# A transformer front end whose adaLN modulation goes through TensorE as unsplit weights with two moving columns, and whose attentions are spread between the projections

## The reference, cut to what matters

```python
mod   = silu(c)     @ w_mod + b_mod          # (1, 6*1024): w_mod is 1024 x 6144
mod_c = silu(c_ctx) @ w_mod + b_mod
h  = rms_norm(x,   norm1_g) * (1 + mod[:, 1])   + mod[:, 0]      # 256 x 1024
hc = rms_norm(ctx, norm1_g) * (1 + mod_c[:, 1]) + mod_c[:, 0]
rq, rk, rv, rg, dq, dk, dv = split(h @ w_in)                     # w_in is 1024 x 3072
crq, crk, crv, crg, cdq, cdk, cdv = split(hc @ w_in)
ret  = rms_norm(retention(rope(rq), rope(rk), rv, crk, crv)) * silu(rg)    # 4 heads
diff = rms_norm((softmax(q1 k1) - lam * softmax(q2 k2)) @ [cdv; dv])       # 4 heads
#      with q, k = rope(rms_norm(dq)), rope(rms_norm(dk)), keys and values of ctx ahead
x = x + mod[:, 2] * (concat(ret, diff) @ w_out)                  # w_out is 1024 x 1024
# then: norm2 with mod[:, 3:5], product-key experts, mod[:, 5], and the second block
```

## Time and profile before

| | us |
|---|---|
| median of 3 runs | 1954.08 (1949.49 to 1954.12) |
| the profiled execution's own time | 1954.57 |
| its span | 1952.8 |
| first projection matmul starts | 60.2 |
| output projection starts, ends | 330.6, 354.2 |
| norm2 turned, queries follow from | 369.3 |

### The profile page before, as it was taken

How to read it: one execution, slowest core, us unless ns; L and a number is a source line. 1 busy time by engine, 2 the same in 40 slices (tenths; PEclk the granted TensorE clock), 3 DMA queues, 4 the chain that set the end, 5 groups by cost and what they waited for, 6 DMA issues and landing times.

```text
span 1952.8 us, 32582 instructions
## 1 busy us (share of the span) xinstructions
PE 1761.0 (90%) x13280; PEld 1550.8 (79%) x13280; DVE 1288.8 (66%) x2058; ACT 949.1 (49%) x1218; POOL 218.7 (11%) x100
## 2 busy tenths in 40 slices
PE   3788975799998999999999999899999678999997
PEld 1455744699898888999999989799989557799985
DVE  5769446589988999877775555555452766555555
ACT  6564433455444555444454444544454435554445
POOL 0123400162200000000000000000006344000000
PEclk8889977899998999999999999999998779999998
DMA  7445301344443444544454545445544122455541
GB/s 280 168 158 189 141 7 46 127 152 155 163 150 116 147 147 146 193 173 168 161 191 173 194 157 189 151 167 180 192 175 182 65 86 87 153 199 180 187 173 65
DMA packets 41958, 299.38 MB, mean 153 GB/s; under 512 B 4624, under 2 KB 4752, under 8 KB 6096
## 3 DMA queue, kind: packets, MB, share of 16 engines
q1 hardware_dynamic: 41296, 294.41, 41.8%
q0 software_dynamic: 512, 2.88, 0.4%
HBM read 295.18 MB, written 2.10 MB: 152 GB/s over the span
## 4 chain that ended last, share of the span: by engine, by line
PE 72%; DVE 20%; ACT 6%; issue 1%; DMA 1%; DVEq 0%; ACTq 0%; SPq 0%
PE pb L607 71%; DVE ar L1558 5%; DVE w_lo L1558 4%; ACT ar L1136 2%; DVE ar L1570 2%; ACT w_hi L1136 2%; DVE ar L1563 1%; DVE ar L1888 1%; ACT L1136 1%; DVE sm L1578 1%; DVE ar L1885 1%; DVE ar L1565 1%; DVE fsc L1565 1%; DVE ar L1574 1%; DVE ar L1892 0%
## 5 line engine op out<-in xcount | busy, mean ns | idle before, releaser
L1558 DVE TENSOR_TENSOR w_lo<-raw,w_hi 128x1024 fp32r<-128x1024 f32 x459 | 569.9, 1242 | 271.9 <-ACT w_hi L1136 250.8
L1136 ACT ACTIVATE w_hi<-raw 128x1024 fp32r<-128x1024 f32 x546 | 579.0, 1060 | 342.0 <-PE pb L607 319.6
L607 PE MATMUL pb<-HX,w_hi 128*128 128x256 f32 x3904 | 712.9, 285 | 4.8 <-DVE w_lo L1558 4.7
L607 PEld LDWEIGHTS pb<-HX,w_hi 128*128 128x128 f32 x3904 | 615.7, 193 | 10.6 <-DVE w_lo L1558 2.9
L607 PE MATMUL pb<-HX,w_lo 128*128 128x256 f32 x1952 | 553.9, 284 | 0.0
L607 PE MATMUL pb<-w_hi,HC 128*128 128x512 f32 (+1 forms) x1584 | 508.6, 392 | 4.5 <-DVE w_lo L1558 4.5
L607 PEld LDWEIGHTS pb<-HX,w_lo 128*128 128x128 f32 x1952 | 376.3, 193 | 0.0
L607 PEld LDWEIGHTS pb<-w_hi,HC 128*128 128x128 f32 x1584 | 298.4, 189 | 64.9 <-DVE w_lo L1558 5.5
L1558 DVE TENSOR_TENSOR ar<-ar 128x512 bf16<-128x512 bf16 (+6 forms) x464 | 276.2, 632 | 73.7 <-ACT ar L1136 54.2
L607 PE MATMUL pb<-w_lo,HC 128*128 128x512 f32 (+1 forms) x792 | 308.4, 389 | 0.0
L1136 ACT ACTIVATE ar<-pb 128x512 f32<-128x512 f32 (+2 forms) x237 | 139.3, 588 | 267.5 <-PE pb L607 198.0
(11 more groups left out here) (116 smaller groups left out, 817.0 us busy)
## 6 DMA issues: line engine op xcount, KB each, us to landing
raw<-in_wall SPq DMA_DIRECT2D x273, 1024.0 KB, 4.8
ar<-in_bigrows POOLq DMA_DIRECT2D x2, 1024.0 KB, 5.2
x<-in_x SPq DMA_DIRECT2D x1, 1024.0 KB, 12.6
ar<-in_ctx SPq DMA_DIRECT2D x1, 1024.0 KB, 14.3
ar<-in_dist SPq DMA_DIRECT2D x1, 1024.0 KB, 6.8
ar<-in_keys SPq DMA_DIRECT2D x1, 1024.0 KB, 4.8
x_keep<-x SPq DMA_DIRECT2D x1, 1024.0 KB, 3.8
x<-x_keep SPq DMA_DIRECT2D x1, 1024.0 KB, 8.3
```

Of the source, the lines that this page charges most:

```text
L607: return e.matmul(o, l, r, start=start, stop=stop, skip_group_check=True)
L1136: a.did(e.activation(out, in_, func, scale=scale, **kw), sig)
L1558: v.did(e.tensor_tensor(out, a_, b_, op), sig)
```

## The change

The modulation's weights are no longer split. Each block of 128 output features is eight plain f32 matmuls straight from `raw`: the stationary operand is a 128x128 piece of `w_mod`, the moving one is the two columns silu(c), silu(c_ctx) (`mod_block`). The result is already in columns, so `mrow`, its copies and its transposes go. There are 48 such blocks, 384 matmuls. Only the 24 projection halves (and all later ones) are split now, all of them in the front on VectorE; `reach` says how far the splitting may run ahead past unsplit halves.

The norm's factor is folded into the turning: x and ctx are multiplied with a scaled diagonal `dg4` in plain f32 (`first_turn`) instead of being scaled and transposed. The group order becomes 3, 4, 5, 0, 1, 2 (differential q, k, v first), and the head transposes, the rounds of differential attention, the masks and retention stand between projection halves and modulation blocks (`front_steps`). The output projection takes the differential half of `w_out` first, and retention's norm and transposes come in its middle.

```diff
-GROUPS = [3, 4, 0, 1, 5, 2]
+GROUPS = [3, 4, 5, 0, 1, 2]
...
+    mods(0, 12)
+    steps.append(("xturn", 0))
+    mods(12, 16)
+    steps.append(("gain", 0))
+    win(0, 0, ("cturn", 0))
+    win(0, 1, ("cturn", 1), ("cturn", 2), ("ctx", 0), ("ctx", 1))
...
+    win(2, 3, ("evac", 2), ("square", 5), ("unit", 5))
+    win(3, 0, ("kturn", 0))
+    mods(16, 18)
...
+    mods(22, 24)
+    steps.append(("score", 0))
+    win(3, 2, ("score", 1), ("turn", 0))
+    mods(24, 28)
+    steps.extend([("score", 2), ("weigh", 0), ("turn", 1)])
+    win(3, 3, ("evac", 3), ("score", 3), ("weigh", 1), ("turn", 2))
+    mods(28, 32)
+    steps.extend([("added", 1), ("score", 4), ("weigh", 2), ("turn", 3)])
+    win(4, 0, ("score", 5), ("weigh", 3), ("turn", 4), ("mask", 0))
+    win(4, 1, ("score", 6), ("weigh", 4), ("turn", 5), ("rope", 4))
...
+    win(5, 2, ("rscore", 0), ("dnorm", 0))
+    mods(32, 34)
+    win(5, 3, ("evac", 5), ("rscore", 1), ("rweigh", 0))
+    mods(34, 36)
+    steps.extend([("rscore", 2), ("rweigh", 1)])
+    mods(36, 38)
+    steps.extend([("rscore", 3), ("rweigh", 2)])
+    mods(38, 42)
+    steps.extend([("rweigh", 3), ("dblocks", 0)])
+    mods(42, 48)
+    steps.extend([("added", 2), ("rnorm", 0)])
...
+def front_halves():
+    order = [s for s in FRONT if s[0] in ("mod", "win")]
+    first = [s for s in order if s[:2] == ("win", 0)]
+    rest = [s for s in order if s not in first]
+    at = rest.index(("mod", 12))
+    return rest[:at] + first + rest[at:]
...
-            def mod_half(u, g, hh):
...
-                for kk in range(2):
-                    for p in range(2):
-                        ins = mm(b[0:4, :], c4[:, 2 * hh + kk, :], wv[p][:, kk, :], hh == kk == p == 0,
-                                 hh == 3 and kk == p == 1)
-                t.did(ins, s_used)
-                if hh == 3:
...
-                    for n in range(4):
-                        ins = e.transpose(pm[:, 4 * g + n, :], mrow[0:4, n * 128:(n + 1) * 128], ident[0:4, 0:4])
+            def mod_block(n):
+                u = HALF_OF["mod", n]
+                w = raw_half(u).rearrange("p (k n) -> p k n", k=8)
+                t.wait_ge(*landed(u))
+                t.wait_ge(s_c2, 1)
...
+                for k in range(8):
+                    ins = mm(pm[:, n, :], w[:, k, :], c2v[:, k, :], k == 0, k == 7)
+                t.did(ins, s_modu)
+
+            def first_turn(n, src, dg):
+                for i in range(2):
+                    ins = mm(block_bank(n)[:, i * 128:(i + 1) * 128], src[:, i, n % 8 * 128:(n % 8 + 1) * 128],
+                             dg4[:, dg + i, :], True, True)
+                t.did(ins, s_tr)
...
-            t.wait_ge(s_ex, 16)
-            tok_major(U_OUT1, 8, [0, 1, 2, 3], hl, lambda k: (s_fl, TB_RET + k + 1), N_PEER, row1())
+            def retention_blocks():
+                t.wait_ge(s_yf, 2)
+                for k in range(4):
+                    t.wait_ge(s_ret, k + 1)
+                    block(TB_RET + k, lambda i: y_block(i, k))
...
+            tok_major(U_OUT1, 8, [0, 1, 2, 3], ol, lambda k: (s_fl, TB_DIFF + k + 1), N_PEER, row1(), 1, retention_blocks)
...
+            def added_mods(b):
+                s_ = slice(16 * b, 16 * b + 16)
+                v.wait_ge(s_modu, 16 * b + 16)
+                tt(modT[:, s_, :], pm[:, s_, :], bc(col("bmod")[:, s_], 2, 2), ADD, sig=s_mod)
```

More of the change, by code:

```diff
@@ L134, in front_steps @@
 def front_steps():
[L135 to L156, removed]
@@ L157, in front_steps, with mods, win @@
-    assert u == U_OUT1 and m == 48
+    steps = []
+    def mods(a, b):
+        steps.extend(("mod", n) for n in range(a, b))
+    def win(p, h, *more):
+        steps.append(("win", p, h))
+        steps.extend(more)
+    mods(0, 12)
[4 more added lines that the diff above has]
+    win(0, 1, ("cturn", 1), ("cturn", 2), ("ctx", 0), ("ctx", 1))
+    win(0, 2, ("cturn", 3), ("ctx", 2), ("ctx", 3))
+    win(0, 3, ("evac", 0), ("ctx", 4), ("ctx", 5))
@@ new lines, with reach @@
+HALVES = front_halves()
+assert len(HALVES) == U_OUT1
+HALF_OF = {s: u for u, s in enumerate(HALVES)}
+SPLIT = [u for u in range(U_END) if u >= U_OUT1 or HALVES[u][0] == "win"]
+ORD = {u: n for n, u in enumerate(SPLIT)}
+def reach(u):
+    split = sum(1 for w in SPLIT if w < u)
+    n = split
+    while n < min(split + AHEAD + (u in ORD), len(SPLIT)):
+        needed = range(u, 2 * (SPLIT[n] // 2 - NRAW) + 2)
+        if any(w < U_OUT1 and HALVES[w][0] == "mod" for w in needed):
+            break
+        n += 1
+    return n
@@ new lines, with win_bank, win_free, group_done @@
+WIN_MADE = {(p, i): sum(len(tiles_of(g)) - 1 for g in GROUPS[:p]) + i + 1 for p, g in enumerate(GROUPS) for i in tiles_of(g)}
+def win_bank(p, i):
+    return 2 if GROUPS[p] == 0 and i >= 2 else i
+def win_free(p, i):
+    bank = win_bank(p, i)
+    return max([WIN_EVAC[q, j] for q in range(p) for j in tiles_of(GROUPS[q]) if win_bank(q, j) == bank], default=0)
+def group_done(g):
+    p = GROUPS.index(g)
+    return max(WIN_EVAC[p, i] for i in tiles_of(g))
+TB_X, TB_CTX, TB_DIFF, TB_RET, TB_U, TB_Y = 0, 8, 16, 20, 24, 32
@@ L329, in lows, with read @@
         def lows(u):
[L330 to L334, removed]
+            pool = sum(1 for w in LO_POOL if w <= u)
+            return (s_lop, pool) if u in LO_POOL else (s_lov, ORD[u] + 1 - pool)
+        LOW = {u: lows(u) for u in SPLIT}
         def used(u):
-            return u + 1
+            return ORD[u] + 1
+        def read(u):
+            return LOW[u] if u in ORD else (s_modu, HALVES[u][1] + 1)
         def raw_half(u):
@@ L521, in heads4, with ol @@
             return ap.rearrange("p (h d) -> p h d", d=128)
+        def ol(k, i):
+            return [HC[:, s_, (k + 4) % 8, i * 128:(i + 1) * 128] for s_ in range(2)]
         def hl(k, i):
@@ L828, in tok_major @@
                     after(k)
+                if middle is not None:
+                    middle()
                 last_four([u0 + nk - 4 + n for n in range(4)], banks, lambda n, i: rows_(nk - 4 + n, i), j,
@@ L1281, in scalar_program, with qk_rows @@
+            for i, s in enumerate([x[:, 0, :], x[:, 1, :], ctx[:, 0, :], ctx[:, 1, :]]):
+                act(scr, s, ACT.Square, scale=1.0 / 32, acc=rs[:, i:i + 1])
+            a.wait_ge(s_eps, 1)
+            act(rs, rs, ACT.Sqrt, bias=epsc, sig=s_std)
+            def qk_rows(n):
+                return pj(n, 1536, 2048) if n < 2 else pj(n - 2, 2048, 2560)
+            for name, n, *more in FRONT:
+                if name == "gain":
+                    ahead(HALF_OF["win", 0, 0])
                     for k in range(8):
@@ L1334, in scalar_program @@
-            for k in range(5):
-                ahead(U_OUT1 + k)
+            ahead(U_OUT1 + 4)
             norm(N_PEER, U_OUT1 + 7, scr3)
@@ L1791, in vector_program @@
[L1791 to L1800 removed]
+                tt(ap, s1, s2, ADD, sig=sig)
             def combine(n):
```

835 lines of the change are left out of this document (390 added, 445 removed).

## The result

| | before | after |
|---|---|---|
| median of 9 runs (lowest to highest) | 1955.08 us (1949.41 to 1956.97) | 1961.95 us (1957.91 to 1968.81) |
| ratio, 95% interval | | 1.0044 (1.0027 to 1.0062) |
| span of the profiled execution | 1952.8 us | 1960.2 us |
| first projection | 60.2 us | 69.2 us |
| output projection starts, lasts | 330.57, 23.6 us | 334.92, 31.05 us |

The change made the kernel slower, by 6.9 us in the medians and 7.4 in the traces. The forecast was 1976, 22 us slower.

A forecast was written before the change was run, and what follows sets the result against it. It took the front as held by attention without projections beside it and by VectorE's splits, with TensorE paying for the change. Output projection 18.4 us later plus 3.3 more: 1954.6 + 18.4 + 3.3 = 1976 us, range 1880 to 2000.

The forecast's parts named there:

- A: Stage up to the first projection: 16 modulation blocks (42 and 14 us) and x turned; ends at 74 us, against 60.2.
- C: Stage of projection group 0 with 16 modulation blocks in four runs of 10.5 us, half way between clocks; 84 us, ending at 223.
- E: Stage of projection group 2, with weighing, first retention score and two modulation blocks (3.5 us); 20 us, ending at 280.
- F: The tail before the output projection: 14 modulation blocks (49 us), retention scores and weighing, transposes; 69 us, ending at 349.
- nothing behind 369 is changed: Everything after norm2's turning begins at 369.34 us was taken as unchanged, adding 0 us.
- Records and price at each clock: A modulation block is 16 records at 0.11 us (2.4 GHz) or 0.22 (1.2): 1.75 or 3.5 us.
- Which runs fall: Long runs of modulation blocks go at 1.2 GHz, runs of four between projection halves half way, two behind dense work at 2.4.
- the prediction's own point where the sign flips, 2.8: Average us per modulation block at which slower turns to faster; forecast 3.1 for +22, full-clock rival 1.75 for -74.
- its rule for pairs: Two modulation blocks behind dense work run at 2.4 GHz, a block costing 1.75 us there.
- The full clock: Rival: modulation blocks keep 2.4 GHz, output projection starts at 255.5 us, total 1880 us; chance 0.2.
- The middle case, 1951: Rival: only the long runs in A and F fall, C's groups of four ride at 2.4 GHz; 1951 us, chance 0.15.
- VectorE was no bound: Answers the rival that VectorE stays the bound and TensorE waits in B to D: at worst 1990 us, chance 0.05.

The follow-up runs named there:

- e8_wide: Changed kernel with seven of eight modulation products streaming 128 identity columns past the same loaded weights, their sums left out; 1917.45 us, ratio to before 0.9810.
- e7_pairs: Changed kernel with the last 16 modulation blocks in pairs between the last projections and retention steps, nothing left out; 1957.11 us, ratio to before 1.0027.
- e1_half_k: Also e1: changed kernel with each modulation block multiplying only the first four of its eight pieces; 1901.63 us, ratio to before 0.9716.
- e4: Changed kernel with the modulation split again, the new order of projections and attentions kept; 1929.23 us, ratio to before 0.9865.
- e3_swapped: Changed kernel with operands swapped in seven of eight modulation products (two columns loaded, 128 streamed), their sums left out; 1924.37 us, ratio to before 0.9837.
- e9_filled: Changed kernel with every modulation record streaming 128 columns of the tables' tile instead of two, nothing left out; 1916.76 us, ratio to before 0.9810.

## Why the prediction was wrong

The side, the mechanism and the place were right: TensorE took the front over, the unsplit modulation cost it more (55.6 to 140.2 us) than the order gave, because most of its records came at the pace that the stretches at a clock of 0.50 show, 0.213 us each. The size was not: +22 forecast, +7.4 in the traces. The sum's terms, forecast and measured:

| term of the forecast | forecast | measured | error |
|---|---|---|---|
| modulation, A (16 blocks) | 56 | 52.3 | -3.7 |
| modulation, C (16 blocks) | 42 | 41.4 | -0.6 |
| modulation, E (2 blocks) | 3.5 | 5.8 | +2.3 |
| modulation, F (14 blocks) | 49 | 40.7 | -8.3 |
| other work up to the output projection | 198.5 | 194.7 | -3.8 |
| output projection | 26.9 | 31.05 | +4.1 |
| behind ("nothing behind 369 is changed") | 0 | -4.4 | -4.4 |

Together -14.4 (-20.8 and +6.4, so some of the errors cancelled), and 21.7 less that is 7.3.

- *Records and price at each clock.* Right: 768 records, 0.213 to 0.214 us at the slow pace (0.22 forecast; the clock is 0.50 where the column can be read), 0.107 in the changed kernel (last section) and 0.105 in e8_wide at 1.00 (0.11 forecast). No run shows the clock in GHz, only as a share of full speed: what the forecast has at 2.4 and 1.2 GHz, the runs showed at 1.00 and 0.50. That the price of a two-column record is its weight load was the author's reading; what was measured is that the loads (PEld) were busy 140.6 us beside the matmuls' 140.2, and that 128 columns streamed past the same load cost no more (0.105).
- *Which runs fall.* This is the step that failed by most, and in F: the forecast counted all 14 blocks of the tail as long runs at the low clock (49 us). Two pairs of them stand behind retention steps and cost 3.9 and 4.2 us, not 7 each, 5.9 of the 8.3; the runs of four and six blocks cost 32.6 for 35. In E, the two blocks behind dense work that were to run at the full clock took 5.8: the clock was 1.00 from 250 to 257 us, 0.86 from 257 to 259 and 0.50 from 259 to 263, so it fell within the pair. In C, half way (10.5 us) was the measured value of three groups, and the fourth took 9.7. A block came to 2.92 us on average where the forecast had 3.1; the prediction's own point where the sign flips, 2.8, is not far below, so the outcome was close to a draw. So the step was right that the clock sets the price, as e7_pairs and e8_wide bear out, and wrong in which blocks it gave to which clock; its rule for pairs, the full clock behind dense work, held for most pairs (3.6 to 4.2 us), less well for one in e7_pairs (4.8) and not for the one in E.
- *Stage ends.* A came at 69.2 (74), the start of the output projection at 334.9 (349).
- *The output projection.* Mis-sized by 4: retention's four blocks now stand in its middle, and TensorE waits 4.1 us there for the gate's diagonals (3.0) and HC (1.1), which the forecast put at nothing. The rest, 26.9 us of busy time, is what it had forecast. It is 31.1 to 32.7 us in e1 to e4 too, with the clock at 1.00 ahead of it in some, so it is the new order's, not the clock's.
- *Behind.* The part behind the front was taken as unchanged. It gave 4 us back in both traces of the changed kernel, 0 in e1_half_k to e3_swapped. Runs of one kernel differ by more than that (7.6 us before, 10.9 after; the traced execution of e1_half_k is itself 4.2 above its median), so this term isn't clear of the scatter. Its rows differ in stretches where the clock moves: in the first 100 us behind the last turning it is 1.00 against 0.98, and from 800 to 900 us behind 0.98 against 0.95. Why the same instructions get another clock there is open.
- *Rivals.* The full clock did not come, for the reason given; e9_filled comes near to it, and it gives 1917, not 1880. Its output projection starts at 286.8, not 255.5: its records took 93.8 us for 84, and TensorE then waits for VectorE in the rounds (13.8 us), for the bias add (4.3) and for transfers behind the first wait (4.3), which a sum of TensorE's work alone leaves out. The output projection then takes 8 us more than that rival had. The middle case, 1951, had C too fast. VectorE was no bound: TensorE waits for it 24 us up to 385, and 11.7 of that is norm2, as before.

TensorE is busy 13.70 of the 13.70 us from 294.3 to 308 in the changed kernel at a clock of 0.50, and 4.00 of 4.00 in e8_wide at 1.00, so what the trace counts as busy did not decide the clock.

## What to carry to other kernels

Here a plain f32 record that loaded 128 columns and streamed two cost 0.107 us at a clock of 1.00, as much as with 128 streamed (0.105), and twice that, 0.213, at 0.50. So where a matmul has a few moving columns only, look at the records' spacing in a stretch of nothing else; if it is twice that of the same load elsewhere, try to stream more columns, even useless ones, where they fall on columns that are written later (e9_filled: 46.4 us less of TensorE), or to set other work between (e7_pairs: 8.7 us less). And when a change takes one engine's load away and puts another's in its place, price the two apart: here the order was worth 26 us or more and the modulation's new form took it back, which one number for both would have hidden.

## What the hardware showed that was not expected

- The granted clock stands at 1.00 in the first 50 us of the changed kernel while its records come 0.214 us apart, the pace of the stretches at 0.50 (21 in 4 us against 20); in e8_wide 38 come in 4 us at the same 1.00. The trace's first entry of the clock is a rise to 1.00 at 53.6 us, and the same two-column records on its two sides, both under 1.00 in the column, come 0.21 and 0.107 us apart:

```profile
28.00:48.00 20.00, 20.00 (x95) 1.00 0.45 157
54.30:57.00 2.70, 2.67 (x25) 1.00 1.01 425
```

  Before that entry the column can't be read here; the spacing can. What TensorE did before that rise, from 47.97 us on, was the turning of x, which streams 128 columns a record.
- 128 columns streamed behind a load of 128 cost nothing over two columns at the same clock (0.105 us a record against 0.107 in the second row above, and 0.109 for 16 columns, in fp32r, in the earlier trace rows), and a load of two columns with 128 streamed saved nothing: 0.111 in e3_swapped.
- The rest of the program, unchanged, took from 1574.7 to 1581.4 us in the twelve traces. How much of that comes from what stood ahead of it, and how much from the scatter between executions, no run here tells apart.
